# Output products of a two-block transformer kernel: the two weight blocks of a pair written side by side

## What is computed

```python
# first block
m = hgrn2_mixer(rmsnorm(x, norm_pre_mix), ...)      # u = h @ w_in; recurrence; o @ hgrn_w_out
x = x + rmsnorm(m, norm_post_mix)
x = x + rmsnorm(conv_ffn(h, ffn_w_in, ffn_w_conv, ffn_w_out), norm_post_ffn)   # (silu(gate) * val) @ ffn_w_out
# second block
mixed = concat(stick_breaking_attention(...), gated_deltanet(...))
x = x + mixed @ w_out
x = x + memory_cross_attention(...)                 # o @ w_xo
x = x + (silu(gate) * up) @ w_down
return rmsnorm(x, final_norm)
```

## Time and profile before

| | us |
|---|---|
| median of three runs | 2698.67 |
| lowest and highest | 2698.19, 2699.48 |
| span of the profiled execution | 2698.5 |
| TensorE busy | 2685.8 |
| VectorE busy | 1971.1 |
| ScalarE busy | 1335.1 |
| all L445 to L447 of `acts` (down1, down2), durations | 815.8 |

### The profile page before, as it was taken

One profiled execution on the slowest core, in us unless ns is written; L12 is line 12 of the kernel. 1 busy time (PEld: TensorE's weight loads), 2 busy tenths in 40 slices (PEclk: granted clock), 3 DMA queues, 4 the chain that ended last, 5 costly groups with the idle time before them and its releaser, 6 DMA issues.

```text
span 2698.5 us, 47418 instructions
## 1 busy us (share of the span) xinstructions
PE 2685.8 (100%) x17614; PEld 2294.1 (85%) x17614; DVE 1971.1 (73%) x2720; ACT 1335.1 (49%) x1680; POOL 133.6 (5%) x138
## 2 busy tenths in 40 slices
PE   9999999999999999999999999999999999999998
PEld 8888888888888888888888888878888888888887
DVE  7888888878888888644466677767678888885444
ACT  6455555455444444433465556665644444443443
POOL 0211121210000000000000000000000000000000
PEclk9999999999999999999999999999999999999999
DMA  7555555465555555655645544455455555555554
GB/s 246 179 167 169 165 173 171 161 192 172 187 187 187 187 187 187 194 187 187 218 138 176 171 146 135 134 171 187 150 192 188 187 187 187 187 187 196 185 185 150
DMA packets 136197, 481.68 MB, mean 178 GB/s; under 512 B 14880, under 2 KB 19120, under 8 KB 135680
## 3 DMA queue, kind: packets, MB, share of 16 engines
q1 hardware_dynamic: 134160, 472.06, 53.0%
q0 software_dynamic: 1376, 7.46, 0.8%
q10 hardware_dynamic: 528, 0.26, 0.0%
HBM read 477.63 MB, written 2.10 MB: 178 GB/s over the span
## 4 chain that ended last, share of the span: by engine, by line
PE 89%; DVE 4%; DMA 3%; issue 2%; ACT 1%; DVEq 0%; SPq 0%; ACTq 0%
PE acc L422 34%; PE acc L424 17%; PE acc L445 8%; PE acc L447 8%; PE acc L446 8%; PE acc L393 4%; DMA raw<-stream 3%; PE acc L395 2%; DVE wts L340 2%; ACT wts L334 1%; DVE cy L2294 1%; PE ps L1386 1%; PE ps L720 1%; PE acc L907 1%; DVE cin L371 0%
## 5 line engine op out<-in xcount | busy, mean ns | idle before, releaser
L422 PE MATMUL acc<-hs,wts 128*128 128x512 f32 x4640 | 1627.1, 394 | 0.2
L340 DVE TENSOR_TENSOR wts<-raw,wts 128x1024 fp32r<-128x1024 f32 x888 | 1062.1, 1226 | 524.3 <-ACT wts L334 523.5
L334 ACT ACTIVATE wts<-raw 128x1024 fp32r<-128x1024 f32 x888 | 913.0, 1054 | 849.0 <-PE acc L424 359.5
L424 PE MATMUL acc<-hs,wts 128*128 128x256 f32 x4640 | 1297.1, 280 | 0.0
L422 PEld LDWEIGHTS acc<-hs,wts 128*128 128x128 f32 x4640 | 871.1, 188 | 194.2 <-DVE wts L340 1.4
L424 PEld LDWEIGHTS acc<-hs,wts 128*128 128x128 f32 x4640 | 871.7, 188 | 0.5
L445 PE MATMUL acc<-wts,acts 128*128 128x512 f32 x688 | 272.6, 396 | 1.1 <-DVE wts L340 1.1
L447 PE MATMUL acc<-wts,acts 128*128 128x512 f32 x688 | 272.8, 396 | 0.0
L446 PE MATMUL acc<-wts,acts 128*128 128x512 f32 x688 | 270.4, 393 | 0.0
L348 ACT ACTIVATE half<-acc 128x512 f32<-128x512 f32 x161 | 95.4, 592 | 157.8 <-PE acc L424 138.9
L445 PEld LDWEIGHTS acc<-wts,acts 128*128 128x128 f32 x688 | 129.2, 188 | 32.2 <-DVE wts L340 2.0
(11 more groups left out here) (363 smaller groups left out, 2180.0 us busy)
## 6 DMA issues: line engine op xcount, KB each, us to landing
raw<-stream SPq DMA_DIRECT2D x888, 512.0 KB, 4.1
xf<-xT SPq DMA_DIRECT2D x8, 256.0 KB, 6.4
raw<-stream SPq DMA_DIRECT2D x8, 256.0 KB, 6.5
fm<-memT POOLq DMA_DIRECT2D x2, 1024.0 KB, 6.9
fw<-stream POOLq DMA_DIRECT2D x2, 1024.0 KB, 11.1
memr<-memT POOLq DMA_DIRECT2D x1, 2048.0 KB, 8.7
outT<-memr SPq DMA_DIRECT2D x7, 256.0 KB, 2.9
KQ<-masks POOLq DMA_DIRECT2D x1, 448.0 KB, 5.3
```

Source lines behind the costliest of these rows:

```text
L334: nc.scalar.activation(whi[:, b, :], raw[:, b, :], ACT.Copy).then_inc(hi_ready, 1)
L340: nc.vector.tensor_tensor(wlo[:, b, :], raw[:, b, :], whi[:, b, :].bitcast(F32), ALU.subtract).then_inc(lo_ready, 1)
L422: nc.tensor.matmul(acc[:, 2 * par + n, :], whi[:, b, c:c + P], src[:, kt, :], start=start, stop=False)
L424: mm = nc.tensor.matmul(acc[:, 2 * par + n, 0:T], wlo[:, b, c:c + P], src[:, kt, 0:T], start=False, stop=stop)
```

## The change

Both blocks of a pair are written side by side. In the 2048 words of slots b and b + 1 (b even), `whi` now holds for each q the 256 words of block b and right behind them the 256 words of block b + 1, and `wlo` the same. The helper `beside(ap, b)` is the view of one block in it: four runs of 256 with a step of 512. ScalarE and VectorE write through it, and VectorE reads `whi` through it; the count of instructions and their order stay, on all engines. A matmul of an output product then moves 512 contiguous words (`wide_row`), and its output is the plain bank (`wide_out`).

`joins(lap, k)` says which blocks are written so: all of `hgout`, `mixout` and `xo`, and `down1` and `down2` without their first four. Since a block of such a pair covers half of both slots, `round_hi` of the first block of a pair (b even) waits for `blk_used >= i + 2` where it waited for i + 1.

```diff
+        def joins(lap, k):
+            if not isinstance(lap, int):
+                return False
+            return any(BLOCK_AT[n] + (4 if n in ("down1", "down2") else 0) <= SLOTS * lap + k < BLOCK_AT[n] + count
+                       for n, count in RING if n in WIDE_AT)
+        def by_rows(ap):
+            return ap.rearrange("p (q c) -> p q c", q=4)
+        def pair(ap, b):
+            return ap[:, b - b % 2:b - b % 2 + 2, :].rearrange("p n f -> p (n f)")
+        def beside(ap, b):
+            return pair(ap, b).rearrange("p (q n c) -> p q n c", q=4, n=2)[:, :, b % 2, :]
+        def wide_row(ap, lap, k, kt):
+            r, b = at(lap, k)
+            q = kt % 4
+            if joins(lap, k):
+                return pair(ap, b)[:, q * 512:(q + 1) * 512]
+            return ap[:, b:b + 2, q * 256:(q + 1) * 256]
+        def wide_out(bank, lap, k):
+            return bank if joins(lap, k) else bank.rearrange("p (s n) -> p s n", s=2)
         def round_hi(act, lap, k):
             r, b = at(lap, k)
+            paired = joins(lap, k)
             act.wait_ge(raw_in[b], 16 * r + 16)
-            act.wait_ge(blk_used, SLOTS * r + b + 1)
-            nc.scalar.activation(whi[:, b, :], raw[:, b, :], ACT.Copy).then_inc(hi_ready, 1)
+            act.wait_ge(blk_used, SLOTS * r + b + (2 if paired and b % 2 == 0 else 1))
+            to, of = (beside(whi, b), by_rows(raw[:, b, :])) if paired else (whi[:, b, :], raw[:, b, :])
+            nc.scalar.activation(to, of, ACT.Copy).then_inc(hi_ready, 1)
         def take_lo(dve, lap, k):
             r, b = at(lap, k)
             dve.wait_ge(hi_ready, SLOTS * r + b + 1)
-            nc.vector.tensor_tensor(wlo[:, b, :], raw[:, b, :], whi[:, b, :].bitcast(F32),
-                                    ALU.subtract).then_inc(lo_ready, 1)
+            if joins(lap, k):
+                nc.vector.tensor_tensor(beside(wlo, b), by_rows(raw[:, b, :]), beside(whi, b).bitcast(F32),
+                                        ALU.subtract).then_inc(lo_ready, 1)
+            else:
+                nc.vector.tensor_tensor(wlo[:, b, :], raw[:, b, :], whi[:, b, :].bitcast(F32),
+                                        ALU.subtract).then_inc(lo_ready, 1)
...
@@ weigh_wide; last_pairs in the same way
-                out = acc[:, 2 * par + c, :].rearrange("p (s n) -> p s n", s=2)
+                out = wide_out(acc[:, 2 * par + c, :], lap, k)
                 for q, kt in enumerate(kts):
-                    w = slice(kt % 4 * 256, (kt % 4 + 1) * 256)
+                    high_w, low_w = (wide_row(ap, lap, k, kt) for ap in (whi, wlo))
                     high, low = src[:, kt, c * P:(c + 1) * P], src[:, kt, T + c * P:T + (c + 1) * P]
-                    nc.tensor.matmul(out, high, whi[:, b:b + 2, w], start=start and q == 0, stop=False)
-                    nc.tensor.matmul(out, high, wlo[:, b:b + 2, w], start=False, stop=False)
-                    mm = nc.tensor.matmul(out, low, whi[:, b:b + 2, w], start=False,
+                    nc.tensor.matmul(out, high, high_w, start=start and q == 0, stop=False)
+                    nc.tensor.matmul(out, high, low_w, start=False, stop=False)
+                    mm = nc.tensor.matmul(out, low, high_w, start=False,
                                           stop=stop and q == len(kts) - 1)
```

## The result

The changed kernel takes **2704.36 us** (median of 13 runs, 2703.10 to 2706.04). The kernel before took 2699.33 (13 runs, 2698.19 to 2700.24). The ratio is 1.002 with a 95% interval of 1.0013 to 1.0027: slower by 0.2%, some 5 us. The forecast was 2693.2, in a range that ended at 2698.7, so it was wrong in size and in sign. The profiled execution has a span of 2703.5 us, 5.0 more than before. One of the seven executions of one kernel further down (the change without its longer wait, with 96 bytes of room) ran at a granted clock of 0.85 and took 2912.23 us, and is left out of that kernel's median.

What follows compares the result with a forecast made beforehand. TensorE, busy 2685.8 of 2698.5 us, was taken as the bound. Jumps -9.6, mixout +3.1 and xo +1.0 gave -5.5, so 2693.2 us; own case 2691.9 to 2696.2, range 2687.8 to 2698.7 (0.82).

Steps and rivals of the forecast that it cites:

- The last two differ in two jumps, and take 6.6 ns more: 3.3 ns a jump.: L422 with L424 against L393 with L395, 1536 columns each: the break between two moved runs was priced at 3.3 ns.
- term of -9.6 us: On TensorE, 2880 output-product matmuls each lose one break between moved runs, at 3.33 ns: 9.6 us less.
- The start of an instruction and the start of a run inside one seem to cost alike.: On TensorE, per 1536 columns: four runs 693.3, six runs 700.0, so three runs should take 690.
- three stretches: Steady TensorE stretches, each brought to 1536 columns: L445 to L447 0.7000 us, L422 with L424 0.6934, L393 with L395 0.7000.
- range of 2.9 to 3.8 ns: Price of one break between moved runs, from the printed hundredths of L393 with L395: 8.3 to 10.9 us saved.
- rival 2: TensorE pitch depends on columns and surroundings, not runs; only the added waits remain: 2698.7 + 4.1 = 2702.8 us; chance 0.10.
- bound of 5.8 us: Most that the added waits at hgout, mixout and xo could cost together: 3.25 + 1.58 + 1 = 5.8 us.
- the entries: TensorE waits where products start, from roundings waiting one block longer: mixout 3.1 us, xo 1.0, hgout 0.
- the base: Starting time of the sum: the span 2698.5 was said to agree with the median 2698.67 within 0.2.
- the mask: At hgout, a late VectorE mask might eat the 1.2 us to spare before TensorE reads `AO`; cost at most 1 us.
- Rivals 3 and 4: 3: VectorE's four-run writes set the pace, 2795 us, chance 0.06. 4: the joined form is not taken, no chance.

## Why the prediction was wrong, step by step

- **"The last two differ in two jumps, and take 6.6 ns more: 3.3 ns a jump." This step failed.** The measured price is 0, at 2880 and at 2736 matmuls, and at all three placements where it was tried. The comparison was of two stretches that had the same columns and as many instructions, but the activations were in the stationary role in one and moved in the other. With the roles held fixed, couples took 0.700 with a jump and 0.700 without, and 0.693 with the roles changed. The whole term of -9.6 us goes, which is what made the sign wrong.
- **"The start of an instruction and the start of a run inside one seem to cost alike." Wrong**, and testable in one run: an extra run costs 0, and an extra instruction, with the activations stationary, 0 (four instead of three for 1536 columns) or 6.7 ns (a matmul cut in two). It was what made three stretches fit one formula: two unknown prices and only three numbers, at least two of which go with the place of tiles as well.
- **The range of 2.9 to 3.8 ns** was the rounding of printed hundredths, not the doubt about the cause. That the price could be nothing was known, as rival 2, and should have been inside the range. With it and the bound of 5.8 us on the entries the range would have ended at 2698.7 + 5.8 = 2704.5.
- **Rival 2 came true in its first half**: pitch does not depend on runs. It does depend on more than columns, on the place of the tiles. Its 2702.8 is 1.6 under the median, of which 0.7 is its base (2698.67 from three runs, 2699.33 from thirteen) and 0.9 the entries, and it had a chance of 0.10. The Trainium skill, TensorE: Matmul & The Clock Gate, section Back-to-back issue gap, has no term for runs, and none was found here. It gives 215.8 ns for 512 columns only as the isolated gap of a matmul, which the prediction did not say; for a stream of weight loads and matmuls it gives about 131 ns. Neither was seen: the undisturbed stretches have 226.7 to 234.3.
- **A small slip in the base.** The prediction takes it that the span, 2698.5, agrees with the median, 2698.67. In all the runs of the changed kernel the time is some 1.8 us more than the span, so the profiled execution took about 2700.3. The sum starts at 2698.7, the median, and is not touched by it.
- **The entries were right**: mixout 3.26 against 3.1, xo 1.28 against 1.0. hgout was 0.54 against 0, within the bound of 1 but through VectorE's `sql` instead of the mask, and was made up later. 5.1 us of stalls in all, of which 4.5 stay, against 4.1 and a bound of 5.8, and the run with the wait alone confirms the mechanism by itself. That the stalls add up to the 5.0 us of the medians is partly luck: the last 0.5 us of the trace come from elsewhere.
- **Rivals 3 and 4 rightly had small chances or none**: a rounding takes 1055 ns on ScalarE and 1231 on VectorE, and the 240 low parts in four runs show that the new form is taken. The roundings of a pair in `down1` take 2.01 and 2.36 us, to the hundredth those of the earlier trace rows:

```profile
1184.03 2.01 ACT L367 ACTIVATE wts<-raw 128x1024 fp32r<-128x1024 f32 x2 [3.59 <-PE acc L484]
```

```profile
1185.12 2.36 DVE L374 TENSOR_TENSOR wts<-raw,wts 128x1024 fp32r<-128x1024 f32 x2 [3.24 <-ACT wts L367]
```

## What to carry to other kernels

A difference of a few nanoseconds between two stretches of a trace is a price only if nothing else differs between them; where it is multiplied by thousands, keep zero in the range or measure it first. An added wait is priced well by following the queue behind it, on every engine that it delays, up to the next product. And where TensorE is the bound, try a few dozen bytes of unused room between the tiles of weights and activations, for one kind of matmul at a time: here that gave 17.7 us, where the change was hoped to give 5.5.

## What the runs showed of the hardware

- At the granted clock of 2.4 GHz, a float32 matmul of 512 columns with its own weight load started every 226.7 ns when both operands lay in one tile, and every 226.7 to 234.3 ns when they lay in two, by which was stationary and where they lay. Room of 96 bytes under the tiles above `hold` took 0.63% off the kernel; room of 64 bytes below `hs` as well added 0.8% (one run).
- Moved operands in two runs of 256 words, 4 KB apart, cost TensorE the same as one run of 512. Cutting such a matmul in two cost 6.7 ns (0.720 us against 0.700 for three).
- Writing 1024 words in four runs of 256 cost ScalarE nothing (1053 ns a block against 1056 in the same trace) and VectorE about 5 ns in 1226.
- The place of tiles can hide or imitate the effect of a change that moves what follows in memory. The kernels compared here have the same layout, except where room was put in on purpose.
